# One decoder step on one Trainium2 core: attention as one loop over row tiles, with changes in the memory, output and expert stages

## The reference

```
mk = mem_prompt @ w_k;  mv = mem_prompt @ w_v          # (256, 1024), prompt only
y, conv, s = token_mixer(rmsnorm(x, nm), ...)          # projection w_in, conv, GLA, @ w_out
x = x + y
x = x + mem_attend(rmsnorm(x, nmem), mk, mv, wq, wom)  # samples use their own cache_mem_k/v
x = x + hier_moe(rmsnorm(x, nf), ...)                  # top 1 of 4 groups, top 2 of 4 experts
y = rmsnorm(x, norm_final)

def mem_attend(h, mk, mv, w_q, w_o):
    q = (h @ w_q).reshape(Bn, T, 4, 256)
    s = einsum('bthd,bmhd->bhtm', q, mk) * 256 ** -0.5
    p = softmax(s)                                     # over 256 memory tokens
    o = einsum('bhtm,bmhd->bthd', p, mv).reshape(Bn, T, 1024)
    return o @ w_o
```

## Time and profile before

| | us |
|---|---|
| median of three runs | 1247.71 |
| the profiled execution | 1250.03 |
| its span, first to last instruction | 1248.1 |
| TensorE busy | 1152.6 (92%) |
| VectorE busy | 447.8 (36%) |
| ScalarE busy | 370.5 (30%) |
| GpSimd busy | 105.8 (8%) |
| mean granted clock of TensorE | 0.946 of full speed |

### The profile page before, as it was taken

The page is one execution under the profiler, slowest core; times in us unless marked ns, Lnnn a source line. Parts: engine busy times, 40 slices in busy tenths (PEclk is TensorE's granted clock), DMA queues, the critical chain, the costliest instruction groups (busy, mean ns, idle before and its releaser), DMA issues.

```text
span 1248.1 us, 13898 instructions
## 1 busy us (share of the span) xinstructions
PE 1152.6 (92%) x5806; PEld 864.0 (69%) x5806; DVE 447.8 (36%) x733; ACT 370.5 (30%) x553; POOL 105.8 (8%) x118
## 2 busy tenths in 40 slices
PE   6898978999999998999999888989999699999994
PEld 5678978888888887888799653437886554444441
DVE  4644230444344434432210365324224522222222
ACT  4545232211211114221211212233112025545542
POOL 1000000000000000000000000000000124444433
PEclk9999989998999979999999878999999599999997
DMA  7470111011101213421213142434321898887721
GB/s 228 185 219 20 49 43 42 18 34 35 35 18 34 73 51 135 135 92 62 70 35 140 63 159 93 148 114 164 115 108 68 315 420 303 335 331 306 296 93 49
DMA packets 86105, 163.26 MB, mean 131 GB/s; under 512 B 20354, under 2 KB 57490, under 8 KB 79636
## 3 DMA queue, kind: packets, MB, share of 16 engines
q1 hardware_dynamic: 71636, 136.91, 30.8%
q0 software_dynamic: 14400, 25.40, 5.9%
HBM read 140.84 MB, written 48.50 MB: 152 GB/s over the span
## 4 chain that ended last, share of the span: by engine, by line
PE 84%; DVE 7%; ACT 4%; issue 2%; DMA 1%; POOL 0%; DVEq 0%; POOLq 0%; ACTq 0%; SPq 0%
PE G L1242 16%; PE G L1182 11%; PE G L1184 10%; PE G L1183 10%; PE G L703 9%; PE G L725 4%; PE G L1538 2%; PE G L707 2%; PE G L1494 2%; PE T L1257 2%; PE T L1510 2%; PE T L695 2%; PE T L1424 2%; PE G L1510 1%; PE G L1288 1%
## 5 line engine op out<-in xcount | busy, mean ns | idle before, releaser
L1182 PE MATMUL G<-act_hi,w_hi 128*128 128x344 f32 (+1 forms) x792 | 264.7, 334 | 16.8 <-DVE w_lo L1837 6.2
L1183 PE MATMUL G<-act_lo,w_hi 128*128 128x344 f32 (+1 forms) x792 | 257.7, 325 | 0.0
L1184 PE MATMUL G<-act_hi,w_lo 128*128 128x344 f32 (+1 forms) x792 | 257.4, 325 | 0.0
L1182 PEld LDWEIGHTS G<-act_hi,w_hi 128*128 128x128 f32 (+1 forms) x792 | 151.0, 191 | 29.5 <-issue 19.9
L1242 PE MATMUL G<-wt,act_hi 128*128 128x512 f32 (+1 forms) x576 | 161.8, 403 | 7.9 <-DVE act_lo L2060 4.9
L1183 PEld LDWEIGHTS G<-act_lo,w_hi 128*128 128x128 f32 (+1 forms) x792 | 151.1, 191 | 2.6 <-issue 1.2
L1184 PEld LDWEIGHTS G<-act_hi,w_lo 128*128 128x128 f32 (+1 forms) x792 | 150.8, 190 | 1.4
L1242 PEld LDWEIGHTS G<-wt,act_hi 128*128 128x128 f32 (+1 forms) x576 | 103.1, 181 | 39.9 <-issue 9.0
L703 PE MATMUL G<-wring,misc 128*128 128x512 f32 x256 | 114.5, 601 | 1.2 <-ACT misc L772 1.2
L600 POOL DMA_INDIRECT misc<-d_h,tidx x20 | 20.7, 1036 | 1008.7 <-DVE tidx L916 980.1
L1242 PE MATMUL G<-wt,act_lo 128*128 128x512 f32 (+1 forms) x288 | 91.5, 399 | 0.0
(11 more groups left out here) (323 smaller groups left out, 1447.0 us busy)
## 6 DMA issues: line engine op xcount, KB each, us to landing
wring<-in_w_gate_dram SPq DMA_DIRECT2D x16, 1024.0 KB, 11.3
wring<-in_w_up_dram SPq DMA_DIRECT2D x16, 1024.0 KB, 13.6
wring<-in_w_down_dram SPq DMA_DIRECT2D x16, 1024.0 KB, 16.4
arena<-in_w_in_dram SPq DMA_DIRECT2D x24, 512.0 KB, 3.8
arena<-in_x_prompt_dram SPq DMA_DIRECT2D x16, 512.0 KB
d_x<-arena SPq DMA_DIRECT2D x16, 512.0 KB
arena<-in_cache_mem_k_dram SPq DMA_DIRECT2D x8, 1024.0 KB, 4.9
arena<-in_cache_mem_v_dram SPq DMA_DIRECT2D x8, 1024.0 KB, 4.9
```

Source lines behind the costliest of these rows:

```text
L1182: pe.matmul(out, a_hi, b_hi, start=first, stop=False)
L1183: pe.matmul(out, a_hi, b_lo, start=False, stop=False)
L1184: return pe.matmul(out, a_lo, b_hi, start=False, stop=last)
```

## The change

The order rows below name an engine's instructions in program order: line, operation, output<-inputs, shape, count.

```
-    FWD_AFTER = (1, 3, 4, 5, 6, 9, 11, 13, 14)
-    KEYS_T = (10, 12)
+    FWD_AFTER = (1, 3, 4, 5, 6, 8, 10, 12, 14)
+    KEYS_T = (11, 13)
...
-    order += [("att", t) for t in range(NT // 2)]
-    order += [("smax", 0), ("pv", 0), ("sprob", 0)]
-    order += [("att", NT // 2 + t) for t in range(NT // 2)]
-    order += [("sout", 0), ("pv", 1)]
-    order += [("split", at[("o", k)]) for k in range(KB)]
-    order += token_stage(2)
+    PAIRS, UP = NT // 2, KB // 2
+    KEYS_OF = {0: (0, 6), 1: (0, 8), 2: (5, 5), 3: (5, 5), 4: (5, 5), 5: (5, 5), 6: (5, 5)}
+    order += [("caches", 0), ("sq", 0), ("sc", 0), ("max", 0), ("exp", (0, 0, MH)), ("sc", 1), ("rc", 0), ("scl", 0), ("kload", 0)]
+    for t in range(NT):
+        pv = [("pvk", n) for n in range((t - 2) * UP // 2, (t - 1) * UP // 2)] if t >= 2 else []
+        more, k0, k1 = t + 1 < NT, *KEYS_OF.get(t, (0, 0))
+        order += [("max", t + 1)] * more + [("tr", t)] + keys(k0) + [("exp", (t + 1, 0, 2))] * more + pv[0:1]
+        order += [("exp", (t + 1, 2, MH)), ("rc", t + 1)] * more + pv[1:2] + [("scl", t + 1)] * more + keys(k1)
+        if t + 2 < NT:
+            order.append(("sc", t + 2))
+    tail = [("pvk", n) for n in range((NT - 2) * UP // 2, PAIRS * UP)]
+    order += [("smax", 0)] + tail[0:2] + [("sprob", 0), ("val", 0), ("val", 1), ("vload", 0)] + tail[2:4]
+    order += [("val", 2), ("val", 3), ("val", 4), ("vload", 1)] + [("split", at[("o", k)]) for k in range(KB // 2)]
+    own = token_stage(2)
+    order += own[0:1] + [("val", b) for b in range(5, DB)] + [("sout", 0), ("gain3", 0)]
+    order += [("split", at[("o", k)]) for k in range(KB // 2, KB)]
+    order += own[1:2] + [("sout", 1)] + own[2:]
...
@@ SyncE @@
+                elif what == "kload":
+                    for b in range(2, DB):
+                        sp.wait_ge(s["q_sc"], b - 1)
+                        sp.dma_start(qb[b % 2], d_q[b].partition_broadcast(P)).then_inc(s[f"kc_in{b % 2}"], 16)
                         sp.dma_start(cache[b % 2], cache_mem_k[0, b].rearrange("(m p) h d -> p m (h d)", p=P)).then_inc(s[f"kc_in{b % 2}"], 16)
+                        if b < 4:
+                            load_values(sp, b - 2)
+                    for b in range(2, 5):
+                        sp.wait_ge(s["q_sc"], DB - 1 if b == 2 else DB)
+                        load_values(sp, b)
...
@@ TensorE, token_rows @@
+                if t == NT:
+                    for k in range(KB):
+                        for half in range(2):
+                            for c in range(2):
+                                ins = pe.matmul(OUT[t % 2][0:XLO + DB, c, :], xs[:, k, :], wt[:, j + half, c * 512:(c + 1) * 512],
+                                                start=(k == 0 and half == 0), stop=(k == KB - 1 and half == 1))
...
@@ TensorE @@
+                elif what == "val":
+                    pe.wait_ge(*values_in(i))
+                    for m in range(MB):
+                        for h in range(MH):
+                            r = slice(h * DB * MH, (h + 1) * DB * MH)
+                            ins = pe.matmul(own_at[r], pTz[:, m, i, :], caches[V_IN[i]][:, m, h * DH:(h + 1) * DH],
+                                            start=(i == 0 and m == 0), stop=(i == DB - 1 and m == MB - 1))
...
@@ ScalarE @@
-                    elif what != "end" and i + 1 < NBLK and not by_rows[i + 1]:
-                        split_hi(i + 1)
+                    if mem_row[i]:
+                        if i + 2 <= 2 * KB:
+                            split_hi(i + 2)
...
+                elif what == "scl":
+                    for h in range(MH):
+                        ins = act.activation(pr[i % 2][:, h, :], pr[i % 2][:, h, :], ACT.Identity, scale=smx[:, i % 2, 3, h:h + 1])
...
@@ VectorE, residual @@
+                if t == NT:
+                    link(v.tensor_tensor(x3, OUT[t % 2][XLO:XLO + r], x3, ALU.add))
                 v.tensor_tensor(x3, OUT[t % 2][0:r], x3, ALU.add).then_inc(s["res_done"], 1)
...
@@ GpSimd, expert stage @@
-                scatter_out(st)
+                if st > NG:
+                    scatter_out(st)
+                if st % 4 == 2 and st + 2 < MAIN:
+                    pool.drain()
```

More of the change, by code:

```diff
@@ L549, in all_out @@
                 eng.wait_ge(s[f"acc_out{b}"], 16 * len(range(b, n, 2)))
-                eng.wait_ge(s[f"y_out{b}"], 32 * len(range(b, n, 2)))
+                eng.wait_ge(s[f"y_out{b}"], 32 * len([t for t in range(b, n, 2) if t > NG]))
         def sp_moe(sp):
@@ L1332, in _ @@
                     for k in range(KB):
[L1333 removed]
+                        ins = pe.transpose(edge[k // 4][:, (k % 4) * P:(k % 4 + 1) * P], mtm[0][:, i, k * P:(k + 1) * P], ident[:, :])
                     ins.then_inc(s["mem_tr"], 1)
@@ L1465, in _ @@
+                    ins.then_inc(s["own_tr"], 1)
                 elif what == "sprob":
@@ L1541, in _ @@
+                    for k in range(DH // P):
+                        ins = pe.transpose(T[:, 1, k * P:(k + 1) * P], so[:, k * P:(k + 1) * P], ident[:, :])
+                    ins.then_inc(s["own_tr"], 1)
             pe_moe(pe)
@@ L1691, in _ @@
                 elif what in ("block", "begin", "end"):
-                    if what != "end" and i + 1 < NBLK and not by_rows[i + 1]:
+                    if mem_row[i]:
+                        if i + 2 <= 2 * KB:
+                            split_hi(i + 2)
+                    elif what != "end" and i + 1 < NBLK and not by_rows[i + 1]:
                         split_hi(i + 1)
@@ L1786, in _ @@
                     for b in range(DB):
                         ins = act.copy(pTz[:, :, b, b * MH:(b + 1) * MH],
-                                       back[:, 1, 0:MB * DB * MH].rearrange("p (m e) -> p m e", m=MB)[:, :, b * MH:(b + 1) * MH])
+                                       own_at[:, 0:MB * DB * MH].rearrange("p (m e) -> p m e", m=MB)[:, :, b * MH:(b + 1) * MH])
                     ins.then_inc(s["q_pT"], 1)
+                elif what == "sout" and i == 0:
+                    act.wait_ge(s["q_o"], DB)
+                    act.copy(so, own_at).then_inc(s["so_ev"], 1)
@@ L1938, in _ @@
                 elif what in ("block", "begin", "end"):
-                    if what != "end" and i + 1 < NBLK and not by_rows[i + 1]:
+                    if mem_row[i]:
+                        if i + 2 <= 2 * KB:
+                            split_lo(i + 2)
+                    elif what != "end" and i + 1 < NBLK and not by_rows[i + 1]:
                         split_lo(i + 1)
```

451 lines of the change are left out of this document (234 added, 217 removed).

## The result

The changed kernel takes 1194.63 us (median of 4 runs, 1189.23 to 1195.59), the kernel before 1248.33 us on the same chip: ratio 0.9563, 95% interval 0.9532 to 0.9595, so faster by 53.7 us. The forecast was 1189 (1175 to 1207) with 59.8 us gained. The profiled execution took 1195.59 us, with a span of 1193.6 against 1248.1.

A forecast was written before the change was run, and what follows sets the result against it. TensorE was taken as busy nearly throughout, except in the memory stage and attention's first half. Gains of 7 (memory), 46.7 (attention) and 6.1 (output projections), 59.8 us, from 1250.0 gave 1190.2, less 2.3 about 1188; forecast 1189, range 1175 to 1207.

The forecast's parts named there:

- (a): Attention's start: scores of tile 0, then the first two tiles as a chain with nothing to fill it, 25.0 us.
- (e): Attention's start: 2.4 us added for TensorE's lower clock in (a).
- (b, f): Attention loop: five tiles of 8.3 us, 41.5 us; plus waits for key loads, 3.6 us at 6.5 us per load.
- rival (1): Attention loop goes at the pace of its DMAs, 9.2 us per sample's keys: 14 us back, 1203 us; chance 0.16.
- Values: Attention: one sample's values in four column groups take 1.3 us, between 0.9 and 1.75, before 3.55.
- `w_o` waits: First output projection's first two tiles: waits for `w_o` blocks, whose fourth load stands behind 1 MB of values, 3.5 us.
- rival (3): Attention: TensorE's clock stays low through small stops in each tile, making the kernel slower, 1260 us; chance 0.04.
- Memory stage: Memory stage: three TensorE waits, 6.05 us, and some slow clock go; 7 us gained, bounds 0 and 12 us.
- Rival (2): Memory stage is bound by arrival of its loads, so its 7 us do not come: 1196 us; chance 0.12.
- Stage 1: First output projection: 16 products fewer gain 3.7 us, the added VectorE addition costs nothing.
- Stage 2: Second output projection: 16 products fewer gain 3.7 us, less 1.25 us for the added addition on the path.
- The drains' bounds: Expert stage: GpSimd's drains cost between 0 and 12 us, taken as 0 since GpSimd is idle over half of each step.

The follow-up runs named there:

- the last version: Changed kernel with weight loads one block earlier, constant loads spread, `w_o` casts and loads earlier, query rows loaded before all keys: 1165.76 us, ratio 0.9354.

## Why the prediction was right, and where it was not

- **The sign and most of the size: attention.** Forecast from first score to first residual: 97.8 + 19.7 (the first output tile) = 117.5 us. Measured 114.3. The start (a) with its slow clock (e) was 23.9 us (696.16 to the maximum at 720.09), forecast 27.4. The five tiles with their key waits (b, f) took 43.5 us, to the last key operation at 763.6; forecast 45.1. What follows to the first residual took 46.9, forecast 45.0. The errors are small, and part of them cancels.
- **Inside those: key waits.** Forecast 3.6 us in sum at 6.5 us per load; the loads took 6.8 to 8.7, and VectorE waited 7.1 us, where the prediction's sign was less than 4. Taking the rows away was worth 7.8. The loop still took less than my sum because a tile costs less than 8.3 us: 7.3 to 7.8 in the last version, and 36.4 us for the five here without the key waits. The two errors partly cancel. In the range between "the row's load hides" and "they add up", the truth was nearer to adding up, which rival (1) had. The estimate from the Trainium skill's DMA: Bandwidth & Descriptors (Anatomy of one DMA), 5.6 us for both transfers, was further off than mine; for 1 MB alone it gives 4.4 us, and the row here shows 5.3. The section fits its figure to DMAs that GpSimd issues, and these are SyncE's, which the prediction did not say.
- **Values.** Three samples take 2.80 us in 48 records (the changed kernel's L1591), 0.93 us each, the lower bound; I took 1.3. Four column groups at once ran at the rate of one full-width product, with no visible cost for the narrow weight loads. The rule in TensorE: Matmul & The Clock Gate (Part 3: Packing small matmuls) of the Trainium skill, that a weight load overlaps only when its row group differs, would have made it 1.3; this trace does not agree.
- **`w_o` waits.** I had 3.5 us; TensorE idled 5.2 us for the blocks, and the products behind the first wait ran slower (four in 2.08 us instead of 1.09, at a granted clock of 0.50 from 792.18 to 795.10 us). Moving two casts and loads ahead brought the way to the first residual down by 8.0 us, 4.5 of them these waits.
- **Clock.** 0.97 in the loop, as step (b) and the argument against rival (3) had it. Behind the loop there was a slow piece that no term had: the 16 value records at 764.57 us took 5.35 us, at a granted clock of 0.65, where others take 3.6.
- **Memory stage: the step that failed, by 11.6 us.** I wrote "Bounds: 0 (arrival replaces each wait) and 12 us", took 7, and made arrival a rival with 0.12. Rival (2) had the cause in part: the blocks did come late, but because they were asked for late. Two errors. The lower bound was not low enough, for a lead can also lengthen the loop; and I argued with TensorE's waits and the casts' durations, not with who asks for a load and behind what. The raw ring kept three buffers while the casts moved one block ahead, so a load had one block less to arrive in. The clock, from which I had hoped to win 0.9 us, went the other way: 0.82 from 24 to 56 us and 0.90 from 56 to 84 us, against 0.89 and 1.00. With the load moved as well, the stage was done at 99.6, 4.65 us ahead of the profiled 104.25: most of the 7.
- **Output projections.** Stage 1 as forecast (3.7). Stage 2 gained 0.3 of 2.4: I looked at what waits for the tile, and not at what stood beside it and would outlast it.
- **Expert stage and the end.** Its steps kept their length (-0.84 us), as forecast. The drains' bounds, 0 and 12 us of cost, left out that a drain can gain: 5 to 6 us. Their cost was 0 because TensorE does not wait for GpSimd, not because the stops are short: the first alone is 12.7 us.

By the table the errors were -11.6 (memory), +0.8 (stage 1), +3.1 (attention), -2.1 (stage 2), -1.7 (routing and expert stages) and +6.2 (the end). They sum to -5.3, the distance between 59.8 forecast and 54.5 found in the span. That the sum came this close is luck in good part: the end of the run, which had no term, gave back half of the memory stage's error.

What stays open: why the granted clock falls more often in one execution than in another of nearly the same kernel, as from 311 to 361 us, and how the end of the run depends on the place of the last drain. No run tried either. The slow value unit behind the loop (5.35 us) is gone in the last version, where every group of 16 such records takes 3.6 to 3.7 us.

## What to carry to other kernels

If work on an engine is moved ahead, move its loads ahead by the same distance, and read the loop that a load closes: who must finish before it is asked for. Before crediting fewer instructions on one engine, list what another engine does under their cover, for that is what the path becomes. Two transfers for one consumer should be priced as their sum until a row shows otherwise; the smaller one can often go first, into a place that is needed later.

## What the runs showed of the hardware

- With GpSimd's indirect DMAs in the last stage, the end of the run came 8.7 to 9.9 us behind the last write's issue without drains, and 3.6 to 4.2 with one or four in the loop. Behind the first of four drains GpSimd stood still for 12.7 and 13.2 us, behind the others for 2.6 to 3.7, and for 6.7 behind a single one.
- 8 products (16 records) with 32 stationary columns in four groups and 256 moving columns took 0.93 us, 58 ns per record (2.80 us for 48), at full clock.
- A 512 KB broadcast of one row beside 1 MB of keys lengthens the landing of the keys from 5.3 to 8.2 us.
- TensorE at the same 2.95 us of idle time took 47.9, 49.4 or 51.0 us for the same instructions, at a mean granted clock of 0.96, 0.93 or 0.90.
